# The 48 later conditioning slabs stand every two and a half chunks of the input projection, no longer every third

## The reference

```
mod = silu(c) @ w_ada + b_ada                      # (1 + 8 rows) x 12288
shift1, scale1, gate1, shift2, scale2, gate2 = split(mod, 6)
h = rmsnorm(x, norm1_g) * (1 + scale1) + shift1
qa, ka, va, qb, kb, vb, r, glr = split(h @ w_in)   # 2048 x 6160
oa = dilated windowed attention(qa, ka, va)        # 16 heads of 64; samples use caches of 1024 rows
ob = gated linear attention(qb, kb, vb, log_a)     # 4 heads, state 128 x 256
x = x + gate1 * (concat(norm(oa), norm(ob) * silu(r)) @ w_out)
h2 = rmsnorm(x, norm2_g) * (1 + scale2) + shift2
g, u = split(h2 @ w_up); y = (silu(conv3(g)) * u) @ w_down
x = x + gate2 * y
```

## Time and profile before

| | |
|---|---|
| median of 3 runs | 1656.5 us (1655.76 to 1656.68) |
| the profiled execution | 1655.58 us, span 1654.0 us |
| PE busy | 1612.3 us (97%) |
| DVE, ACT busy | 891.0 us (54%), 719.2 us (43%) |
| DMA, mean over the span | 224 GB/s |

### The profile page before, as it was taken

The page is one execution under the profiler, slowest core; times in us unless marked ns, Lnnn a source line. Parts: engine busy times, 40 slices in busy tenths (PEclk is TensorE's granted clock), DMA queues, the critical chain, the costliest instruction groups (busy, mean ns, idle before and its releaser), DMA issues.

```text
span 1654.0 us, 29469 instructions
## 1 busy us (share of the span) xinstructions
PE 1612.3 (97%) x12258; PEld 1445.7 (87%) x12258; DVE 891.0 (54%) x1562; ACT 719.2 (43%) x1026; POOL 75.2 (5%) x132
## 2 busy tenths in 40 slices
PE   8999999999999889999999999999999999999997
PEld 4778888888888544998999999999999999999997
DVE  3555555455665443644754555545555466656563
ACT  3332444445555433534533433334333345555452
POOL 2000000000111000000000000000000000000000
PEclk8999999999999999999999999999999999999999
DMA  9998777778877999675845445454454545545550
GB/s 342 372 379 314 260 248 240 274 266 288 280 251 273 339 380 351 220 241 171 288 148 177 162 155 180 150 182 158 154 181 157 177 132 178 187 159 173 174 171 34
DMA packets 276113, 370.71 MB, mean 224 GB/s; under 512 B 8273, under 2 KB 192947, under 8 KB 275977
## 3 DMA queue, kind: packets, MB, share of 16 engines
q1 hardware_dynamic: 232928, 279.88, 50.6%
q10 hardware_dynamic: 35970, 71.45, 12.1%
q0 software_dynamic: 7088, 17.54, 3.2%
HBM read 358.96 MB, written 9.88 MB: 223 GB/s over the span
## 4 chain that ended last, share of the span: by engine, by line
PE 84%; issue 5%; DVE 4%; DMA 3%; ACT 2%; SPq 1%; POOL 0%; ACTq 0%; DVEq 0%; POOLq 0%
PE ps L921 23%; PE ps L922 22%; PE ps L923 22%; PE ps L872 4%; PE ps L1168 2%; DMA ring<-in_w_in 1%; PE ps L1183 1%; SPq L525 1%; PE ps L1213 1%; DMA vals<-in_w_ada 1%; DMA proj<-in_w_ada 1%; PE ps L879 1%; DVE wlo L1995 1%; ACT whi L1470 0%; PE ps L1097 0%
## 5 line engine op out<-in xcount | busy, mean ns | idle before, releaser
L921 PE MATMUL ps<-hhi,whi 128*128 128x288 f32 x3136 | 934.7, 298 | 1.4 <-DVE hlo L1987 0.7
L922 PE MATMUL ps<-hlo,whi 128*128 128x288 f32 x3136 | 921.9, 294 | 0.0
L923 PE MATMUL ps<-hhi,wlo 128*128 128x288 f32 x3136 | 921.8, 294 | 0.0
L921 PEld LDWEIGHTS ps<-hhi,whi 128*128 128x128 f32 x3136 | 588.3, 188 | 40.0 <-issue 33.4
L922 PEld LDWEIGHTS ps<-hlo,whi 128*128 128x128 f32 x3136 | 588.5, 188 | 0.9
L923 PEld LDWEIGHTS ps<-hhi,wlo 128*128 128x128 f32 x3136 | 588.4, 188 | 0.0
L1856 DVE TENSOR_TENSOR wlo<-ring,whi 128x1024 fp32r<-128x1024 f32 x178 | 212.1, 1222 | 85.8 <-ACT whi L1453 85.4
L1453 ACT ACTIVATE whi<-ring 128x1024 fp32r<-128x1024 f32 x178 | 184.6, 1057 | 156.4 <-PE ps L923 156.4
L1995 DVE TENSOR_TENSOR wlo<-ring,whi 128x1024 fp32r<-128x1024 f32 x96 | 117.3, 1224 | 124.0 <-ACT whi L1470 123.9
L1470 ACT ACTIVATE whi<-ring 128x1024 fp32r<-128x1024 f32 x96 | 100.8, 1052 | 137.6 <-PE ps L923 112.7
L2484 DVE TENSOR_TENSOR wlo<-ring,whi 128x1024 fp32r<-128x1024 f32 (+1 forms) x94 | 105.7, 1131 | 56.0 <-ACT whi L1778 56.0
(11 more groups left out here) (312 smaller groups left out, 1184.4 us busy)
## 6 DMA issues: line engine op xcount, KB each, us to landing
ring<-in_w_up SPq DMA_DIRECT2D x88, 1024.0 KB, 5.1
ring<-in_w_ada ACTq DMA_DIRECT2D x58, 1024.0 KB, 8.4
ring<-in_w_in SPq DMA_DIRECT2D x48, 1024.0 KB, 9.2
ring<-in_w_down SPq DMA_DIRECT2D x32, 1408.0 KB, 6.7
ring<-in_cache_k_win SPq DMA_DIRECT2D x16, 1024.0 KB, 9.8
vals<-in_cache_v_win SPq DMA_DIRECT2D x32, 512.0 KB, 8.3
ring<-in_w_out SPq DMA_DIRECT2D x16, 1024.0 KB, 6.0
proj<-in_w_ada SPq DMA_DIRECT2D x14, 1024.0 KB, 10.7
```

The costliest lines, as they stand in the source:

```text
L921: mm(out, w_hi, x_hi, start=start, stop=False)
L922: mm(out, w_hi, x_lo, start=False, stop=False)
L923: return mm(out, w_lo, x_hi, start=False, stop=stop)
```

## The change

`LATE_AT` runs from chunk 22 to 79, no longer to 91:

```diff
-        LATE_AT = [22 + r // 2 * 3 for r in range(48)]
+        LATE_AT = [22 + r // 2 * 5 // 2 for r in range(48)]
```

## The result

| | before | after |
|---|---|---|
| median | 1656.45 us (1655.76 to 1656.68, 4 runs) | 1675.42 us (1674.24 to 1676.38, 4 runs) |
| ratio to before, 95% interval | | 1.0118 (1.0105 to 1.0131) |
| profiled execution | 1655.58 us, span 1654.0 | 1676.38 us, span 1674.8 |

The change costs 19.0 us, 1.2%. I had said +10, 1666.5 in a range of 1658 to 1676: the direction and the range hold, the size is half of what came. The median lies 0.6 us inside the range's upper end, which had been put there for rival A and its 16 us of waits for loads; what came was another sum, so that the range held is in part luck.

A forecast was written before the change was run, and what follows sets the result against it. PE, busy 97%, was taken as the bound, with the pairs' ACT and DVE chain about equally long from chunk 82. 7.6 - 2.2 + 5.0 = +10.4 us on 1655.6 gave 1666.0, stated as 1666.5, range 1658 to 1676.

The forecast's parts named there:

- rival A: Later slabs' loads: all eight tight gaps stall, couples 1 to 3 us late each, 12 to 20 us, 1677; chance 0.10.
- Part 1: End of the later slabs' stretch: 9.0 us of PE work moves ahead, the end shortens by only 1.4; +7.6 us.
- Part 2: Heads: PE's waits for DVE go at chunks 48, 54 and 60, about +0.4 comes at 46; sum -2.2 us.
- Part 3: Short gaps between couples: slab loads late behind chunks 39 and 54, 0.4 us at 47 to 49; +5.0 us.
- rival D: PE's clock might fall at a new gap at chunk 54, +1.7 us, 1667.7; widens the range only, no separate chance.
- Rival B: End of the stretch gives back all 9.0 us, ACT and DVE at half load; 1653.4 to 1658.4, no change; chance 0.13.
- Rival C: Samples' part is bound by DMA, so keys leaving 16 us earlier shorten it by 6.9 us; faster; chance 0.05.

## Why the prediction was half the size

In the profiled executions, step by step:

| term | forecast | measured | from |
|---|---|---|---|
| Part 1, moved work less what the end gives back | +7.6 | +7.8 | 9.0 less (72.0 less 70.8) |
| Part 2, gaps in the heads | -2.2 | -1.8 | 3.3 us before, 1.18 + 0.30 after |
| Part 3, late loads | +5.0 | +9.1 | L872's waits |
| rival D, clock | range only | +4.6 | the windows at 250 and 340 |
| sum | +10.4 | +19.7 of 20.8 | |

1.1 us is not assigned by a row. It belongs to the late loads or their falls: with small loads 14.8 us went and not 13.7, and 9.0 less 1.8 then left nothing over. Each of the six waits also breaks a run of overlapped matmuls, and the 4.6 is an estimate; either may be it, and no run tells.

**Part 1 held, and by its mechanism.** The turns of 20.05, 20.25, 20.25 and 10.05 us came as 19.9, 20.2, 20.2 and 10.4. The gaps at L1121, L1097 and L1107 of pairs 5 to 7 sum to 6.9 us, in the 6 to 8 that I had named, each ended by the DVE line named. The two experiments with cheap slabs show the cause by themselves: 0.6 to 0.9 against 6.2 us.

**Part 2 held in sum, and not in its places.** The gaps at 48, 54 and 60 went. That at 36, which was to stay, went too; a turn now stands in chunk 35, and the likely reading is that it gives DVE the time. At 46 I put a turn that stands in 45, where it covers nothing, so the wait was 1.18 us and not 0.4:

```profile
297.06 0.66 PE L1039 MATMUL ps<-con,proj 128*128 128x128 f32 x4 [1.18 <-DVE proj L2142]
```

Another 0.30 came at chunk 38, where a turn had left; I had not looked there.

**Part 3 is the step that failed by size.** The two places that I named are the two worst (39: 3.3 for 1.7; 54: 2.6 for 2.9), so reading a load's time from the same place was right for one and low for the other. For 39 I kept the landing time of before, 10.6 us, and the second load took 12.4 after, since the state's read now starts with it. I did not move POOL's state traffic against the couples', though PE's order says where it goes. And I took 0 for 29, 69 and 79, "most are in time" by the median of 7.9 us. That median mixes two kinds. Of the 23 couples of the kernel before that were loaded between 150 and 530 us, the first load took 5.4 us at the median (4.9 to 11.0) and the second, issued 0.4 to 0.9 us later, 8.7 (6.9 to 13.9). With 8.3 to 10 us allowed, the second load is at its limit in the ordinary case, and the first only in the rare one. Five of the eight were late (27, 37, 52, 67, 77), and 47 not among them; in all five the second slab was, and behind 54 the first as well.

**Rival D was no rival but a term.** I priced a fall at 1.7 us, said a gap of 3 us might bring it, forecast a 2.9 us gap, and still left it out of the sum. A gap of 3.3 us and one of 2.6 in two pieces came, and the clock fell at both, for 1.7 and 3.4 us. The small loads show that these falls go when the waits go. Rival D also took the fall at 615 for the trace's only one; the clock of the kernel before is below 1.00 in its first 30 us too (0.86 from 10 to 20, 0.63 from 20 to 30).

**Rival A** (1677) had L872 waiting in six or more places as its sign. It is six waits in five places, just short, and the time is nearer to A than to my 1666.5. Its sum was another one, 16 us of waits; 9.1 came, and the clock brought the rest. **Rival B** fell, by 0.9997. **Rival C** fell: SP no longer waited at L617 and sent the first keys 38.5 us ahead of the first L1168 (at 528.46), not 23.5 as before (at 522.74), yet the samples' part took as long as before. So a DMA share of 1.00 there did not mean that earlier keys shorten it.

## To carry to other kernels

Work on the busiest engine is only worth its time where that engine's own work is the longest chain: follow one period from anchor to anchor, and if another chain is as long, filler work in it is free and costs its full time anywhere else. When a load gets less time, set the margin against the slow landings and against the slower of two loads that start together, and redo the overlap of every other queue that moves against it; a mean DMA share of 0.76 says nothing on 10 us at 1.07. A wait of 2 us or more on TensorE is to be priced with the clock fall behind it, as a term of the sum.

## What the runs showed of the hardware

- The granted clock behind gaps on PE, between 150 and 550 us: each of the seven single gaps of 2.0 us and more (3.27, 3.27, 2.48, 2.25, 2.24, 2.05, 2.03, in six kernels) was followed by a stretch at 1.2 GHz, 0.83 in a window of 10 us, so 1.7 us lost. So was each of three close pairs of gaps (1.01 and 1.62, 1.35 and 1.64, 0.60 and 1.80), for 3.4, 3.4 and 1.7 us. No gap at L872 of 1.5 us or less brought one by itself. The Trainium skill (TensorE: Matmul & The Clock Gate, What's actually happening) has the lower level after idleness, and the traces agree. It is not idleness alone: the clock also fell with PE busy throughout (0.66 from 260 to 265 in the kernel with the two couples moved, behind matmuls of 9 and 32 columns), and twice in the pairs, behind two gaps of 0.9 us that brought none in other kernels (0.83 from 490 to 500 in the one with small loads; 0.95 and 0.88 from 490 to 510 in the one with both states small).
- 1 MB loads from HBM landed in 4.9 to 13.9 us. Of two issued at most 0.9 us apart the second took longer, 8.7 against 5.4 us at the median. The second load of the couple for chunk 49, issued at the same place in four kernels, took 13.9, 14.6, 14.9 and 15.1 us. Two side by side with a 1 MB state being read took 5.8 and 12.4 us, with a 1 MB state being written 10.1 and 11.9.
